# Hybrid recurrent decoder step on one core: five projection quanta moved from the row-scale place of five middle blocks to the last block of the first phase

## The reference

```
h    = rmsnorm(x) * (1 + sc1) + sh1                  # modulation from c @ w_ada
proj = h @ w_in                                      # 1024 -> 3208 columns
o_hg = HGRN2(q, f, i of proj) ; y_mb = conv + Mamba-2 SSD(z, xBC, dt of proj)
o_rw = RWKV-7(r, k, v, w, a, g of proj)              # token shift, low-rank gates, state recurrence
x    = x + g1 * (concat(o_hg, y_mb, o_rw) @ w_out)
x    = x + g2 * ((silu(h2 @ w_gate) * (h2 @ w_up)) @ w_down) ;  y = rmsnorm(x)
```

## Time and profile before

| | us |
|---|---|
| median of 3 runs | 1936.76 |
| lowest and highest | 1924.67 and 1938.64 |
| the profiled execution, its own time | 1930.92 |
| its span, first to last instruction | 1929.1 |
| TensorE busy, whole span | 1645.1 (85%) |
| VectorE busy | 979.2 (51%) |
| ScalarE busy | 587.4 (30%) |
| GpSimd busy | 256.1 (13%) |
| mean granted TensorE clock | 0.914 of 2.4 GHz |

### The profile page before, as it was taken

One profiled execution on the slowest core, in us unless ns is written; L12 is line 12 of the kernel. 1 busy time (PEld: TensorE's weight loads), 2 busy tenths in 40 slices (PEclk: granted clock), 3 DMA queues, 4 the chain that ended last, 5 costly groups with the idle time before them and its releaser, 6 DMA issues.

```text
span 1929.1 us, 32185 instructions
## 1 busy us (share of the span) xinstructions
PE 1645.1 (85%) x13599; PEld 1489.4 (77%) x13599; DVE 979.2 (51%) x2112; ACT 587.4 (30%) x1055; POOL 256.1 (13%) x333
## 2 busy tenths in 40 slices
PE   4899998888998185778788887999969999999995
PEld 2898887777886143457677787988969999999995
DVE  5414447776553456766766535555552332423334
ACT  2313233323331321233443333334332222222222
POOL 3501111111000312123233440000000000000000
PEclk9899999889998566668889998999989999999998
DMA  8111011111100433432112243343312231322211
GB/s 302 44 48 30 24 29 35 41 41 43 48 34 9 156 99 125 151 96 74 53 39 83 76 136 91 105 123 103 113 50 66 64 99 45 100 64 68 84 49 55
DMA packets 199302, 149.23 MB, mean 77 GB/s; under 512 B 6479, under 2 KB 187200, under 8 KB 198136
## 3 DMA queue, kind: packets, MB, share of 16 engines
q1 hardware_dynamic: 188482, 120.67, 20.8%
q0 software_dynamic: 7728, 23.27, 3.5%
q10 hardware_dynamic: 2950, 3.24, 0.5%
HBM read 134.03 MB, written 13.18 MB: 76 GB/s over the span
## 4 chain that ended last, share of the span: by engine, by line
PE 69%; DVE 18%; ACT 6%; issue 3%; DMA 2%; POOL 0%; SPq 0%; POOLq 0%; DVEq 0%; ACTq 0%
PE bank L1261 17%; PE bank L1262 17%; PE bank L1263 17%; PE bank L1200 3%; ACT WHI L1825 1%; PE bank L1652 1%; PE bank L1653 1%; PE bank L1488 1%; PE bank L1487 1%; PE bank L1433 1%; PE bank L1426 1%; PE bank L1283 1%; PE bank L1435 1%; PE bank L1584 1%; PE bank L1403 1%
## 5 line engine op out<-in xcount | busy, mean ns | idle before, releaser
L1261 PE MATMUL bank<-HBH,WHI 128*128 128x328 f32 (+1 forms) x832 | 261.1, 314 | 14.8 <-DVE HBL L2384 10.1
L2267 DVE TENSOR_TENSOR WLO<-RAW,WHI 128x1024 fp32r<-128x1024 f32 (+4 forms) x149 | 152.3, 1025 | 235.9 <-ACT WHI L1825 235.4
L1825 ACT CAST WHI<-RAW 128x1024 fp32r<-128x1024 f32 (+4 forms) x210 | 187.9, 898 | 245.3 <-PE bank L1263 237.0
L1262 PE MATMUL bank<-HBL,WHI 128*128 128x328 f32 (+1 forms) x832 | 259.6, 312 | 0.0
L1263 PE MATMUL bank<-HBH,WLO 128*128 128x328 f32 (+1 forms) x832 | 258.7, 311 | 0.0
L1261 PE MATMUL bank<-HHI,WHI 128*128 128x344 f32 x568 | 190.5, 335 | 10.3 <-DVE HLO L2480 6.2
L1022 POOL TENSOR_TENSOR WLO<-RAW,WHI 128x1024 fp32r<-128x1024 f32 (+1 forms) x61 | 131.6, 2159 | 456.0 <-ACT WHI L1825 456.0
L1262 PE MATMUL bank<-HLO,WHI 128*128 128x344 f32 x568 | 184.3, 324 | 0.0
L1263 PE MATMUL bank<-HHI,WLO 128*128 128x344 f32 x568 | 184.2, 324 | 0.0
L1261 PEld LDWEIGHTS bank<-HBH,WHI 128*128 128x128 f32 x832 | 157.1, 189 | 16.0 <-issue 15.8
L1263 PEld LDWEIGHTS bank<-HBH,WLO 128*128 128x128 f32 x832 | 157.3, 189 | 0.0
(11 more groups left out here) (579 smaller groups left out, 3199.1 us busy)
## 6 DMA issues: line engine op xcount, KB each, us to landing
RAW<-in_w_gate SPq DMA_DIRECT2D x44, 512.0 KB, 3.9
RAW<-in_w_up SPq DMA_DIRECT2D x44, 512.0 KB, 3.9
RAW<-in_w_ada SPq DMA_DIRECT2D x32, 512.0 KB, 4.1
RAW<-in_w_in SPq DMA_DIRECT2D x26, 512.0 KB, 3.8
ADAW<-in_w_ada SPq DMA_DIRECT2D x8, 1024.0 KB, 19.9
RAW<-in_w_out SPq DMA_DIRECT2D x16, 512.0 KB, 4.4
RAW<-in_w_down SPq DMA_DIRECT2D x32, 256.0 KB, 2.7
RAW<-in_w_down SPq DMA_DIRECT2D x16, 384.0 KB, 3.5
```

The costliest lines, as they stand in the source:

```text
L1261: mm(bank[:, 0:w], whi[:, k, :], hi_k, start=(k == 0), stop=False)
L1262: mm(bank[:, 0:w], whi[:, k, :], lo_k, start=False, stop=False)
L1825: a.copy(w_split(i)[0][:, 0:nk, :], RAW[u % NRAW][:, 0:nk, :]).then_inc(w_hi, 1)
L2267: v.tensor_tensor(wlo[:, 0:nk, :], RAW[u % NRAW][:, 0:nk, :], whi[:, 0:nk, :].bitcast(F32), ALU.subtract).then_inc(w_lo, 1)
```

## The change

The place behind rs gets no quantum where the rs is that of block 2, 3, 4, 5 or 6. These items stand in the blocks 1 to 5. Three more places get a quantum in the last block alone: behind inv1, inv3 and inv4 of block 7. Since `fill1` and `spread` draw from one queue, every quantum from 39 on comes later, by one place in block 1 up to five places in block 6, and its split, its eviction and its convolution come with it. The places behind turn1 and turn2 and the spread place of block 7, empty or nearly so before, then get quanta as well.

```
         BEHIND = {'turn1': 1, 'turn2': 1, 'lin': 1, 'gates': 1, 'rs': 1, 'decay': 1}
+        LAST = ('inv1', 'inv3', 'inv4')
...
-            fill1(BEHIND.get(item[0][3:], 0))
+            if item[0][3:] in LAST:
+                fill1(item[1] == NB - 1)
+            elif item[0] != 'rw_rs' or not 1 < item[1] < 7:
+                fill1(BEHIND.get(item[0][3:], 0))
```

## The result

The changed kernel takes 1947.8 us (median of 11 runs, 1940.8 to 1954.6) where the kernel before took 1930.3 in the runs beside it (median of 11): a ratio of **1.0075, 95% interval 1.0059 to 1.0091**, about 14.5 us slower. That is a change of less than 1%, and it lies in the stated range. The profiled execution has a span of 1939.0 us instead of 1929.1.

What follows compares the result with a forecast made beforehand. TensorE was taken to bound blocks 1 and 5, VectorE's work and a lowered clock blocks 2 to 4, the bare inverse chain block 7. -5.3 + 10.8 = +5.5 us on a mean of 1932.7 gave 1938 us, range 1914 to 1954.

Steps and rivals of the forecast that it cites:

- Level cover: Levels of the inverse: a quantum behind a level is worth 3.0 us, covered 6.25 against bare 3.21.
- The wait for UV: TensorE waiting for VectorE's UV at L1480: 4.8 us in blocks 2 to 4, 1.1 in blocks 1 and 5.
- Block 7 and the tail: Last block: four newly covered places cost +12.2 us, spread pieces -0.1; tail -1.3 from a faster clock.
- Blocks 2 to 4: Rs places emptied there: block 2 -2.4 us, block 3 -5.1, block 4 +4.0, slow clock behind each wait.
- second part of a block: Merge of level 4 to block end, blocks 2 to 4: 21.1 - 3.0 + 4.8 + 4.8 = 27.7 us.
- Blocks 1 and 5: -1.9 us each: Emptied rs place saves 3.0 us, a new wait for UV costs 1.1, in each of these blocks.
- Part 1: Rs place emptied in blocks 1 to 5: -5.3 us in sum.
- part 2: Block 7 taking the extra quanta, with the tail: +10.8 us in sum.
- The slower rival: Clock falls behind shorter waits too, 23 us more, 1956 us; chance 0.13.
- four short waits: New or moved waits: for UV in blocks 1 and 5 (1.1 us), for a level's merge in blocks 3 and 4 (1.7).
- The clock rival: Waits for UV in blocks 2 to 4 about 2.6 us or less, clock stays up: 1914 us; chance 0.17.
- Cover is all that counts: Rival: blocks 1 to 5 each give 3.0 us, block 7 takes 10.8: -4.4, 1928 us; chance 0.12.

## Why the prediction was right, and where it was off

- **Level cover, 3.0 us per quantum: right.** Covered 6.25, bare 3.21, in both kernels and in the run with one quantum moved alone.
- **The wait for UV: right in size and cause.** Forecast 4.8 in blocks 2 to 4 and 1.1 in blocks 1 and 5, measured 4.9, 4.9, 5.2 and 1.2. Taking out the split lowered it by 2.2, taking out the convolution by 3.7, as the chain was added up.
- **Block 7 and the tail: right.** +12.2 and -1.1 against +12.1 and -1.3.
- **Blocks 2 to 4: a term mis-sized by 0.9 us twice over.** I took block 1's end at 281.5, the transposes of turn1, but its beginning at 228.4, the L1403 behind them. Its true length is 54.0 (the earlier trace rows cut it at 53.1). So the second part of a block is 22.0 - 3.0 + 4.9 + 5.7 = 29.6 us and not 27.7, measured 29.5, 29.5 and 29.9. The slow stretch costs 5.7 us up to the next L1407 and not 4.8: 14.4 against 8.7 us. That is 5.8 us over three blocks, of which 2 were given back by first parts that I had put too long. That these errors took each other back in part was luck.
- **Block 5: the step that failed.** "Blocks 1 and 5: -1.9 us each" counted a wait of 1.1 us without a fall of the clock. The wait came, in both. The clock fell behind it in block 5 (12.7 us instead of 8.7 up to the next L1407, so 4.0 more) and not in block 1. The run with 6 idle matmuls in that wait removed it.
- **Sum.** Part 1 came out at +2.4 us and not at -5.3, so even its sign was wrong; part 2 came out at +11.0 against +10.8. The two terms above, 3.7 and 4.0, are nearly all of the 8 us between forecast (+5.5) and the profile's blocks (+13.6). The forecast is a small difference of large terms, and two misses of some 4 us more than doubled it. The direction and the range held; the size did not. That the clock would decide between the cases was stated, and it did.
- **The slower rival came in part.** Of its four short waits, the one for UV in block 5 brought the whole slow stretch, the two for a level's merge in blocks 3 and 4 brought 3.4 us at half the clock each, and the one in block 1 nothing. Its price was also added up wrongly: 23 us more than the forecast is 1961, not 1956, so the range up to 1954 took in 16 of the 23.
- The clock rival did not come. The shorter waits that it assumed would not have been enough either: behind 2.7 us the clock still fell, three times of three, and behind 1.2 and 1.3 us in blocks 2 and 3 of the run with the later convolution. "Cover is all that counts" fell with block 4.
- What the forecast had not seen: with waits filled, the changed order is the better one. The prediction had the parts for it, -15.2 and +10.8, but put them into a rival and let the clock of four blocks hide them. What it had not priced is the split and the c2 convolution that stand together in front of one merge in the order before.

## What to carry to other kernels

Moving a quantum of matmuls from one level to another is a draw by itself, and only a place that waits anyway takes one for nothing. Price above all the wait that the emptied place uncovers on the next engine in line, and the clock behind that wait, which here cost more than the wait (5.7 beside 4.9 us, and 4.0 beside 1.2). Add up the queue of the engine that ends last (here VectorE: decay chain, stalled operation, convolution), before counting any gain on the one that gets free. Work of that engine that is moved out of one wait must have a free place to go to, or it comes back as the next wait. Where a wait can't be removed, idle matmuls in it are a cheap test of what the clock costs, and here they were also a gain.

## What the runs showed of the hardware that was not expected

Behind a wait for UV of 2.7 us or more the granted clock was at half every time: 4.9, 4.9 and 5.2 us in the changed kernel, 2.7, 2.7 and 3.1 with the split moved. Behind 1.0 to 1.3 us it went either way. In the changed kernel it fell in block 5 and not in block 1; in the run with the later convolution it fell in blocks 2, 3 and 5 and not in blocks 1 and 4; behind the same wait in block 4 of the kernel before it held, and behind 1.0 us in block 4 of that order with all waits filled it fell. What tells these cases apart, no run here shows. Once down, it stayed at half for 10 to 16 us behind the wait, although TensorE was busy in every microsecond of them.

A stretch of block 7 before, in pauses under 1 us, had kept the full clock with only 9.26 of 16 us busy (597 to 613), and the clock was lower right behind it, 0.66 from 613 to 624.7. So pauses of this kind are no proof that the clock is safe.
